# An encoder trunk on one core: the first norm by tiles, the first weight slab in halves, and two orders of work in the later norms

## The chip, the cores and the metric

The kernel runs on 1 core of one Trainium2 chip. Its engines are TensorE (PE), VectorE (DVE), ScalarE (ACT), GpSimd (POOL) and SyncE (SP, which only issues transfers). The metric is the device time of one execution in microseconds (us), the median of the runs.

## The reference, cut to what matters

Two layers of an encoder over x (1, 512, 1024), float32. Layer 0 mixes with RWKV-7 and spatial gating, layer 1 with differential attention; each then cross-attends into 256 memory tokens and ends in a gated MLP. Every sub-layer starts with the same norm and a projection:

```python
def rms_norm(x, gain):
    normed = x * lax.rsqrt(jnp.mean(x * x, axis=-1, keepdims=True) + 1e-6)
    return normed * gain

for l in range(2):
    h = rms_norm(x, mix_norm[l])
    if l == 0:
        z = h @ ab_w_in[0]          # (512, 1024) @ (1024, 2944): zf, zu, zv below
        ...
    x = x + memory_cross_attention(rms_norm(x, cross_norm[l]), ...)
    x = x + conv_gated_ffn(rms_norm(x, ffn_norm[l]), ffn_w_up[l], ..., ffn_w_down[l])
```

## The kernel before

**The products.** Weights come in slabs of 512 rows by 512 columns (`WRAW`, 128x2048 in SBUF, two buffers, loaded by SP in order; the load of slab i waits until slab i-2 is split). Each slab is split into a high part `WHI` (ScalarE, L332, rounds to fp32r) and a low part `WLO` = raw - high (VectorE, L338). Activations are split in the same way into `HIS` and `LOS`. A product is three matmuls (L372): high x high, high x low, low x high, each 128x512. A slab is 4 banks of PSUM x 4 steps x 3 = 48 matmuls. A product `zf` has four groups of banks, two slabs (`si` 0 and 1) each; groups use the same PSUM banks 0 to 3, so a group waits until the one before is evacuated. `gemm_pe` runs the matmuls, `gemm_side` the splits and evacuations on the other engines, up to three slabs ahead or to a given `limit`.

**The order.** Each engine runs a program written out by hand (`tensor_program`, `scalar_program`, `vector_program`, `pool_program`); they meet in semaphores that each count one kind of event (`sq`, `var`, `rstd`, `xn`, `tp`, `hi`, `lo` of a norm; `w_hi`, `w_lo` of the splits).

**A norm** works on four tiles of 128 tokens. ScalarE squares and sums a tile (L461, or in halves L499), VectorE makes the variance, GpSimd raises it to -0.5 (L473 for four columns, L505 for one), VectorE scales the tile (`XN`, L481 or L518). TensorE turns it: 8 transposes of 128x128 a tile, channel block k into bank k (L561, L576, L580). When a channel block has all four tiles (`tp`), ScalarE makes its high tile with the gain (L468) and VectorE its low tile (L487); the first matmul waits for the first low tile.

**The head** (norm `n0`) waits for all four sums at once (`norm_dve_front`), then turns channel by channel into banks 4 to 7 twice (`norm_pe`), so the second four wait for the first four low tiles. The gains come as a row tile `VROW`, turned by TensorE (L2067) and copied to `COLS` by VectorE (`setup_dve`, L2082). Four more row tiles are turned behind the norm (L2071) and give the `factors` (`factors_dve`, L2089 to L2098), for which TensorE and ScalarE wait before the first product. GpSimd issues ten loads of constants (`load_constants`, 2.3 MB) when the first weight slab has landed.

**The norms `nf0`, `nf1`, `n1`** follow a product whose last group fills four banks. `norm_tiles_pe` turns tiles 0 to 2 into the four banks that are free, then into the other four (when the last sum `ev` has been added), then tile 3 into all eight, with one `tp` per channel block. At `n1` the product `dn01` is followed by the product `dk`, whose first two slabs are split before the last four sums (L585) are added.

Of the kernel before, what the change touches and what calls it, by code (L numbers as in the profile page):

```python
# [19 lines left out]
F32 = mybir.dt.float32  # L20
# [5 lines left out]
P = 128  # L26
D = 1024
# [63 lines left out]
def build(nc, a, out):  # L91
# [473 lines left out]
    def norm_tiles_pe(T, tag, name, early):  # L565
# [4 lines left out]
        for ks in (range(early, early + 4), range(late, late + 4)):  # L570
            if ks[0] == late:
                e.wait_ge(*at(name, "ev", 2 * NT))
            for t in range(NT - 1):
                e.wait_ge(*at(tag, "xn", t + 1))
                for k in ks:
                    e.transpose(PS[:, k, t * P:t * P + P], XN[:, t, k * P:k * P + P], ident)  # L576
        t = NT - 1
        e.wait_ge(*at(tag, "xn", NT))
        for k in range(DC):
            e.transpose(PS[:, k, t * P:t * P + P], XN[:, t, k * P:k * P + P], ident).then_inc(sem(tag, "tp"), 1)  # L580
# [1481 lines left out]
    def setup_pe(T):  # L2062
# [3 lines left out]
        e.wait_ge(S("v_first"), V_FIRST)  # L2066
        e.transpose(PS[:, 0, 0:P], VROW[0][:, :], ident).then_inc(S("v_tp"), 1)  # L2067
        norm_pe(T, "n0", XN, NT, 4)
        e.wait_ge(S("v_in"), V_IN)
        for i in range(1, 5):  # L2070
            e.transpose(PS[:, 1, (i - 1) * P:i * P], VROW[i][:, :], ident).then_inc(S("v_tp"), 1)  # L2071
# [7 lines left out]
    def setup_dve(V):  # L2079

        V.e.wait_ge(S("v_tp"), 1)
        V.e.tensor_copy(COLS[:, 0:P], PS[:, 0, 0:P]).then_inc(S("cols"), 1)  # L2082
        V.e.wait_ge(S("cols"), 1)

    def factors_dve(V):
# [3 lines left out]
        V.mine(e.tensor_copy(COLS[:, P:5 * P], PS[:, 1, :]))  # L2089
# [42 lines left out]
    norm_shares("n0", NT)  # L2132
# [103 lines left out]
    def scalar_program(A):  # L2236
# [68 lines left out]
    def vector_program(V):  # L2305
# [21 lines left out]
        for l in range(2):  # L2327
# [155 lines left out]
```

## Time and profile before

| what | value |
|---|---|
| median of 3 runs | 1799.59 us (1798.09 to 1802.88) |
| the profiled execution's own time | 1797.6 us |
| its span, first to last instruction | 1795.8 us |
| mean granted TensorE clock | 0.994 of full |
| TensorE busy | 1730.6 us (96%) |
| VectorE, ScalarE, GpSimd busy | 953.6, 767.0, 177.2 us |

A busy time counts an engine's instructions whether or not anyone waits for them. All times in the trace count from the span's start. An instruction's row gives its start, its length and in brackets how long the engine stood before it and who ended that. A row may merge several instructions of one kind (x4); the length is then that of the whole run. Lengths of consecutive matmuls overlap; their pitch is the run's length by their number. In tables of windows the columns are the window's length, the busy us and number of instructions of PE, PEld (weight loads), DVE, ACT and POOL, then the granted TensorE clock (1.00 is 2.4 GHz, 0.50 is 1.2 GHz), the share of DMA engines busy, and GB/s.

### The profile page before, as it was taken

The page shows a single profiled execution, that of the slowest core. Times are in us where ns is not written, and L with a number is a line of the kernel's source. Part 1 is how long each engine was busy: PE and PEld are TensorE (multiplying, and loading weights), DVE is VectorE, ACT ScalarE, POOL GpSimd, SP SyncE. Part 2 cuts the span into 40 slices and gives each one's busy share as a digit, 9 for nine tenths or more (in the row PEclk, how much of TensorE's full clock was granted, in tenths as well). Part 3 has the DMA queues.
Part 4 walks back from the last instruction along what each step waited for, and adds up shares of the span by engine and source line. Part 5 has one row for each costly group of instructions (what it writes and reads, how often), then busy time and mean ns, then how long its engine had stood idle before and what let it go on. Part 6 is the DMA issues. An engine that isn't in the chain of part 4 may idle for free.

```text
span 1795.8 us, 29502 instructions
## 1 busy us (share of the span) xinstructions
PE 1730.6 (96%) x12913; PEld 1421.7 (79%) x12913; DVE 953.6 (53%) x1257; ACT 767.0 (43%) x1180; POOL 177.2 (10%) x179
## 2 busy tenths in 40 slices
PE   6998899999999999999999999999999999999999
PEld 5877787878887788888887887668887788888887
DVE  5478676545353566525644445875434456634552
ACT  4243555535553444314433235874654344412440
POOL 1001322130100000000000121440010000000000
PEclk9999999999999999999999999999999999999999
DMA  7210000143321332232322222003431233232331
GB/s 248 82 48 1 4 4 28 50 149 120 118 94 49 92 94 94 97 103 82 94 94 94 94 94 71 1 1 118 141 109 49 78 94 94 94 114 74 94 105 60
DMA packets 96444, 149.26 MB, mean 83 GB/s; under 512 B 3479, under 2 KB 50170, under 8 KB 96314
## 3 DMA queue, kind: packets, MB, share of 16 engines
q1 hardware_dynamic: 94727, 142.29, 24.4%
q0 software_dynamic: 1296, 4.95, 0.8%
q8 instruction: 102, 1.67, 0.4%
q14 instruction: 28, 0.23, 0.0%
q10 hardware_dynamic: 291, 0.12, 0.0%
HBM read 145.25 MB, written 2.10 MB: 82 GB/s over the span
## 4 chain that ended last, share of the span: by engine, by line
PE 86%; DVE 6%; ACT 4%; issue 2%; DMA 1%; POOL 1%; SPq 0%; POOLq 0%; ACTq 0%; DVEq 0%
PE PS L372 71%; PE PS L1646 1%; PE PS L1615 1%; DVE SS L1939 1%; PE PS L958 1%; PE PS L684 1%; DVE WLO L338 1%; PE PS L1770 1%; PE PS L1109 1%; PE PS L1071 1%; PE PS L1790 1%; DVE AT L1951 1%; ACT WHI L332 1%; PE PS L561 1%; PE PS L1095 1%
## 5 line engine op out<-in xcount | busy, mean ns | idle before, releaser
L338 DVE TENSOR_TENSOR WLO<-WRAW,WHI 128x2048 fp32r<-128x2048 f32 (+1 forms) x131 | 294.5, 2251 | 443.5 <-ACT WHI L332 443.5
L332 ACT ACTIVATE WHI<-WRAW 128x2048 fp32r<-128x2048 f32 (+1 forms) x132 | 248.4, 1882 | 396.7 <-PE PS L372 381.5
L372 PE MATMUL PS<-HIS,WHI 128*128 128x512 f32 x856 | 333.8, 390 | 3.3 <-DVE LOS L487 1.8
L372 PE MATMUL PS<-HIS,WLO 128*128 128x512 f32 x856 | 333.0, 389 | 0.0
L372 PE MATMUL PS<-LOS,WHI 128*128 128x512 f32 x856 | 333.0, 389 | 0.0
L372 PE MATMUL PS<-WHI,HIS 128*128 128x512 f32 x608 | 241.0, 396 | 0.9 <-DVE LOS L487 0.9
L372 PE MATMUL PS<-WHI,LOS 128*128 128x512 f32 x608 | 237.5, 391 | 0.0
L372 PE MATMUL PS<-WLO,HIS 128*128 128x512 f32 x608 | 237.4, 391 | 0.0
L372 PEld LDWEIGHTS PS<-HIS,WHI 128*128 128x128 f32 x856 | 160.7, 188 | 37.3 <-issue 2.4
L372 PEld LDWEIGHTS PS<-HIS,WLO 128*128 128x128 f32 x856 | 160.7, 188 | 33.5
L372 PEld LDWEIGHTS PS<-LOS,WHI 128*128 128x128 f32 x856 | 160.7, 188 | 33.4 <-issue 0.2
L372 PE MATMUL PS<-WHI,GHI 128*128 128x512 f32 x352 | 136.9, 389 | 0.0
L372 PE MATMUL PS<-WHI,GLO 128*128 128x512 f32 x352 | 136.9, 389 | 0.0
L372 PE MATMUL PS<-WLO,GHI 128*128 128x512 f32 x352 | 136.9, 389 | 0.0
L372 PEld LDWEIGHTS PS<-WHI,HIS 128*128 128x128 f32 x608 | 114.7, 189 | 26.8 <-issue 3.4
L372 PEld LDWEIGHTS PS<-WLO,HIS 128*128 128x128 f32 x608 | 114.7, 189 | 24.3
L372 PEld LDWEIGHTS PS<-WHI,LOS 128*128 128x128 f32 x608 | 114.8, 189 | 23.1
L585 DVE TENSOR_TENSOR X<-X,PS 128x512 f32<-128x512 f32 x64 | 43.0, 684 | 68.9 <-PE PS L372 68.8
L372 PEld LDWEIGHTS PS<-WHI,GLO 128*128 128x128 f32 x352 | 66.1, 188 | 13.8
L372 PEld LDWEIGHTS PS<-WHI,GHI 128*128 128x128 f32 x352 | 66.1, 188 | 13.7
L372 PEld LDWEIGHTS PS<-WLO,GHI 128*128 128x128 f32 x352 | 66.1, 188 | 13.7
L1732 ACT ACTIVATE GHI<-SG 128x512 fp32r<-128x512 f32 x44 | 27.8, 632 | 109.0 <-DVE SG L1752 109.0
(302 smaller groups left out, 2389.8 us busy)
## 6 DMA issues: line engine op xcount, KB each, us to landing
WRAW<-ffn_w_up SPq DMA_DIRECT2D x88, 512.0 KB, 4.7
WRAW<-ffn_w_down SPq DMA_DIRECT2D x20, 1024.0 KB, 5.0
WRAW<-cross_wkv SPq DMA_DIRECT2D x16, 1024.0 KB, 5.0
WRAW<-diff_w_in SPq DMA_DIRECT2D x12, 1024.0 KB, 5.1
WRAW<-ab_w_in SPq DMA_DIRECT2D x10, 1024.0 KB, 5.5
WRAW<-cross_wq SPq DMA_DIRECT2D x8, 1024.0 KB, 5.1
WRAW<-cross_wo SPq DMA_DIRECT2D x8, 1024.0 KB, 5.1
X<-x SPq DMA_DIRECT2D x8, 512.0 KB, 5.3
```

Source lines behind the costliest of these rows:

```text
L332: A.e.activation(part(WHI[place(i)], i), part(WRAW[i % 2], i), ACT.Copy).then_inc(S("w_hi"), 1)
L338: V.e.tensor_tensor(part(WLO[place(i)], i), part(WRAW[i % 2], i), part(WHI[place(i)], i).bitcast(F32), ALU.subtract).then_inc(S("w_lo"), 1)
L372: mm = e.matmul(o, l, r, start=(si == 0 and kk == 0 and q == 0), stop=(si == len(steps) - 1 and kk == nk - 1 and q == 2))
L561: mm = e.transpose(PS[:, norm_bank(b0, k), t * P:t * P + P], xn[:, t, k * P:k * P + P], ident)
L585: V.e.tensor_tensor(o, o, PS[:, bank_base(name, gi) + b, :], ALU.add).then_inc(sem(name, "ev"), 1)
L684: mm = e.transpose(PS[:, bank0 + k % 4, t * P:t * P + P], tok[:, t, k * P:k * P + P], ident)
L958: mm = e.matmul(PS[xs(x), b + hh, t * P:t * P + P].rearrange("p (s k) -> p s k", s=2), l[half(hh), d, chunk(t, x)], ar[half(hh), d, 0:2, c ...
L1071: mm = e.matmul(PS[xs(c), 2 * d + (x ^ c), q * CH:q * CH + CH], AI[xs(x), d, u, :], UU[xs(x), d, 2 * q + c, :], start=True, stop=True)
L1095: mm = e.matmul(PS[xs(x), 2 * d + (x ^ c), q * CH:q * CH + CH], TT[xs(c), d, 2 * q + x, :], XX[xs(c), d, 2 * q + (x ^ c), :], start=True, ...
L1109: mm = e.matmul(PS[xs(x), 2 * d + u // 4, (u % 4) * P:(u % 4) * P + P], UU[xs(x), d, u, :], AXT[xs(x), d, u, :], start=True, stop=True)
L1615: mm = e.matmul(PS[:, 4 * (t % 2) + h // 2, (h % 2) * MEM:(h % 2) * MEM + MEM], QFT[:, 2 * h + k, t * P:t * P + P], KFT[:, 2 * h + k, :], ...
L1732: A.e.activation(GHI[2 * gi + b - 2][:, :], SG[b - 2][:, :], ACT.Copy).then_inc(sem(name, "hi"), 1)
```

## The change

**Head.** The sums, variances, powers and scalings of `n0` go tile by tile (`first_norm_dve`, `norm_pool_tiles`). TensorE turns each tile into all eight banks as it comes (`setup_pe`); the gains' row goes into a corner of bank 7. The first slab's high part is made in two halves (`first_hi_act`), its first low half on VectorE, its second on GpSimd (`first_lo`). The first slab's product (`first_slab_pe`) no longer waits for the factors; it waits for each low tile, takes the second half of the slab when GpSimd is done, and turns the other four row tiles between its banks 1 and 2. The factors are made behind the split of slab 2, on VectorE; ScalarE waits for them before the first evacuation. GpSimd issues the constants' loads after its half.

**Norms `nf0`, `nf1`, `n1`.** Only tiles 0 and 1 are turned ahead; tiles 2 and 3 are turned together, channel block by channel block.

**`n1`.** VectorE's limit of splits before the last sums goes down by one slab: the second slab of `dk` is split after the norm's low tiles. ScalarE's limit stays.

```diff
@@ -570,14 +570,16 @@
         for ks in (range(early, early + 4), range(late, late + 4)):
             if ks[0] == late:
                 e.wait_ge(*at(name, "ev", 2 * NT))
-            for t in range(NT - 1):
+            for t in range(NT - 2):
                 e.wait_ge(*at(tag, "xn", t + 1))
                 for k in ks:
                     e.transpose(PS[:, k, t * P:t * P + P], XN[:, t, k * P:k * P + P], ident)
-        t = NT - 1
-        e.wait_ge(*at(tag, "xn", NT))
         for k in range(DC):
-            e.transpose(PS[:, k, t * P:t * P + P], XN[:, t, k * P:k * P + P], ident).then_inc(sem(tag, "tp"), 1)
+            for t in range(NT - 2, NT):
+                if k == 0:
+                    e.wait_ge(*at(tag, "xn", t + 1))
+                mm = e.transpose(PS[:, k, t * P:t * P + P], XN[:, t, k * P:k * P + P], ident)
+            mm.then_inc(sem(tag, "tp"), 1)
 
     def add_residual(V, name):
         def evac(gi, b, n):
@@ -2063,12 +2065,72 @@
 
         e = T.e
         e.wait_ge(S("ident_in"), 16)
-        e.wait_ge(S("v_first"), V_FIRST)
-        e.transpose(PS[:, 0, 0:P], VROW[0][:, :], ident).then_inc(S("v_tp"), 1)
-        norm_pe(T, "n0", XN, NT, 4)
+        for t in range(NT):
+            if t == NT - 1:
+                e.wait_ge(S("v_first"), V_FIRST)
+                e.transpose(PS[:, 7, 3 * P:4 * P], VROW[0][:, :], ident).then_inc(S("v_tp"), 1)
+            e.wait_ge(*at("n0", "xn", t + 1))
+            for k in range(DC):
+                if (t, k) == (NT - 1, DC - 1):
+                    e.wait_ge(S("cols"), 1)
+                mm = e.transpose(PS[:, k, t * P:t * P + P], XN[:, t, k * P:k * P + P], ident)
+                if t == NT - 1:
+                    mm.then_inc(sem("n0", "tp"), 1)
+
+    def first_slab_pe(T):
+
+        e = T.e
+        ready = lambda k: at("n0", "lo", k)
+        e.wait_ge(S("w_first_lo"), 1)
+        bank_pe(e, "zf", 0, 0, 0, [0, 1], hhi, hlo, tokens_out=False, ready=ready)
+        e.wait_ge(S("w_lo"), 1)
+        bank_pe(e, "zf", 0, 0, 0, [2, 3], hhi, hlo, tokens_out=False, ready=ready)
+        bank_pe(e, "zf", 0, 0, 1, range(4), hhi, hlo, tokens_out=False)
         e.wait_ge(S("v_in"), V_IN)
+        e.wait_ge(*at("n0", "lo", 5))
         for i in range(1, 5):
-            e.transpose(PS[:, 1, (i - 1) * P:i * P], VROW[i][:, :], ident).then_inc(S("v_tp"), 1)
+            e.transpose(PS[:, 4, (i - 1) * P:i * P], VROW[i][:, :], ident).then_inc(S("v_tp"), 1)
+        bank_pe(e, "zf", 0, 0, 2, range(4), hhi, hlo, tokens_out=False)
+        bank_pe(e, "zf", 0, 0, 3, range(4), hhi, hlo, tokens_out=False).then_inc(sem("zf", "wused"), 1)
+
+    def first_hi_act(A, h):
+        part_hi = A.e.activation(WHI[0][:, 2 * h:2 * h + 2, :], WRAW[0][:, 2 * h:2 * h + 2, :], ACT.Copy)
+        part_hi.then_inc(S("w_first_hi" if h == 0 else "w_hi"), 1)
+        A.split = h
+
+    def first_lo(E, h):
+        if h == 1:
+
+            E.e.wait_ge(S("w_first_lo"), 1)
+        E.e.wait_ge(S("w_first_hi" if h == 0 else "w_hi"), 1)
+        E.e.tensor_tensor(WLO[0][:, 2 * h:2 * h + 2, :], WRAW[0][:, 2 * h:2 * h + 2, :],
...
+
+    def first_hi_tile_act(A, k):
+        A.e.wait_ge(*at("n0", "tp", k + 1))
+        A.e.activation(HHI[k][:, :], PS[:, k, :], ACT.Copy, scale=col("mix_norm", k)).then_inc(sem("n0", "hi"), 1)
+
+    def first_lo_tile_dve(V, k):
+        V.e.wait_ge(*at("n0", "hi", k + 1))
+        V.e.scalar_tensor_tensor(HLO[k][:, :], PS[:, k, :], col("mix_norm", k), HHI[k][:, :].bitcast(F32),
+                                 ALU.mult, ALU.subtract).then_inc(sem("n0", "lo"), 1)
+
+    def first_var_dve(V, t):
+        V.e.wait_ge(*at("n0", "sq", t + 1))
+        V.e.tensor_scalar(SM[:, 4 + t:5 + t], SM[:, t:t + 1], 1.0 / D, EPS, ALU.mult, ALU.add)\
+            .then_inc(sem("n0", "var"), 1)
+
+    def first_norm_dve(V):
+
+        for t in range(2):
+            first_var_dve(V, t)
+            scale_tile_dve(V, "n0", t)
+        first_var_dve(V, 2)
+        first_var_dve(V, 3)
+        scale_tile_dve(V, "n0", 2)
+        scale_tile_dve(V, "n0", 3)
+        setup_dve(V)
 
     def setup_pool(G):
         G.mine(G.e.memset(SM[:, 24:25], 1e-12))
@@ -2079,14 +2141,14 @@
     def setup_dve(V):
 
         V.e.wait_ge(S("v_tp"), 1)
-        V.e.tensor_copy(COLS[:, 0:P], PS[:, 0, 0:P]).then_inc(S("cols"), 1)
+        V.e.tensor_copy(COLS[:, 0:P], PS[:, 7, 3 * P:4 * P]).then_inc(S("cols"), 1)
         V.e.wait_ge(S("cols"), 1)
 
     def factors_dve(V):
 
         e = V.e
         e.wait_ge(S("v_tp"), 5)
-        V.mine(e.tensor_copy(COLS[:, P:5 * P], PS[:, 1, :]))
+        V.mine(e.tensor_copy(COLS[:, P:5 * P], PS[:, 4, :]))
         V.wait_mine()
 
         V.mine(e.tensor_tensor(SM[:, 200:215], col("ab_shift_prev", 0, 15), col("ab_shift_next", 0, 15), ALU.add))
...
@@ -2195,8 +2257,9 @@
     def tensor_program(T):
         setup_pe(T)
 
-        T.e.wait_ge(S("factors"), 1)
-        gemm_pe(T, "zf", hhi, hlo, tokens_out=False, operand=lambda k: at("n0", "lo", k))
+        first_slab_pe(T)
+        gemm_pe(T, "zf", hhi, hlo, tokens_out=False, operand=lambda k: at("n0", "lo", k),
+                only=[(gi, si) for gi in range(4) for si in range(2) if gi + si > 0])
         gemm_pe(T, "zu", hhi, hlo, tokens_out=False, beside=zu_beside_pe(T))
         rw0_pe(T)
         gemm_pe(T, "zv", hhi, hlo)
@@ -2239,11 +2302,18 @@
 
         load_vectors(A.e, True)
         norm_act_front(A, "n0", X, SQ, NT, arrives=True)
-        split_hi(A, 1)
+        A.e.wait_ge(S("raw_in0"), raw_level[0])
+        first_hi_act(A, 0)
+        first_hi_act(A, 1)
         A.e.wait_ge(S("cols"), 1)
-        norm_act_back(A, "n0", NT, gcol("mix_norm", 0), hhi, 4)
-        A.e.wait_ge(S("factors"), 1)
-        side("zf", zf_act(A), fence)
+        for k in range(DC):
+            first_hi_tile_act(A, k)
+
+        def vectors(s):
+            if s == 1:
+                A.e.wait_ge(S("factors"), 1)
+
+        side("zf", zf_act(A), fence, vectors)
         lambda_act(A)
         side("zu", zu_act(A), fence, zu_beside_act(A))
         rw0_act(A)
@@ -2306,13 +2376,18 @@
         def side(name, evac=None, limit=None, beside=None):
             gemm_side(V, name, split_lo, evac, limit, beside)
 
-        norm_dve_front(V, "n0", X, XN, NT)
-        split_lo(V, 1)
-        setup_dve(V)
-        norm_dve_back(V, "n0", NT, gcol("mix_norm", 0), hhi, hlo, 4, 0, 4)
-        factors_dve(V)
-        norm_dve_back(V, "n0", NT, gcol("mix_norm", 0), hhi, hlo, 4, 4, DC)
-        side("zf", zf_dve(V), fence)
+        first_norm_dve(V)
+        first_lo(V, 0)
+        for k in range(DC):
+            first_lo_tile_dve(V, k)
+        V.e.wait_ge(S("w_lo"), 1)
+        V.split = 1
+
+        def vectors(s):
+            if s == 0:
+                factors_dve(V)
+
+        side("zf", zf_dve(V), fence, vectors)
         lambda_dve(V)
         side("zu", None, fence, zu_beside_dve(V))
         rw0_dve(V)
@@ -2357,15 +2432,15 @@
                 side(f"up{l}{h}", up_dve(V, l, h))
                 if (l, h) == (0, 1):
 
-                    side("dn01", residual_and_norm_dve(V, "dn01", "n1", close=True), gemms["dk"][0][0][1][0] + 1)
+                    side("dn01", residual_and_norm_dve(V, "dn01", "n1", close=True), gemms["dk"][0][0][0][0] + 1)
                 else:
                     side(f"dn{l}{h}", add_residual(V, f"dn{l}{h}"))
 
 
     def pool_program(G):
         setup_pool(G)
-        norm_pool(G, "n0", NT)
-        G.e.wait_ge(S("raw_in0"), 16)
+        norm_pool_tiles(G, "n0")
+        first_lo(G, 1)
         load_constants(G.e)
         rw0_pool(G)
         sgu_pool(G)
```

## Rows read from the trace of the kernel before

**Rows 1.** The page, part 4: the chain that ended last, shares by engine.

```profile
PE 86%; DVE 6%; ACT 4%; issue 2%; DMA 1%; POOL 1%; SPq 0%; POOLq 0%; ACTq 0%; DVEq 0%
```

**Rows 2.** The chain in order of time, 0 to 90 us: start, length, what.

```profile
24.43 65.58 PE PS L372 x288
```

**Rows 3.** Timeline of the head: start, length, engine, line, what [idle before <-releaser].

```profile
5.78 0.19 ACT L461 ACTIVATION_READ_ACCUMULATOR SQ<-X 128x1 f32 x1
...
12.02 2.74 DVE L481 TENSOR_SCALAR XN<-X,SM 128x1024 f32<-128x1024 f32 x4 [1.21 <-POOL SM L473]
...
12.62 1.91 ACT L332 ACTIVATE WHI<-WRAW 128x2048 fp32r<-128x2048 f32 x1 [2.01 <-DMA WRAW<-ab_w_in]
...
16.88 0.29 DVE L2082 COPY COLS<-PS 128x128 f32<-128x128 f32 x1
...
17.20 2.42 ACT L468 ACTIVATE HIS<-PS,COLS 128x512 fp32r<-128x512 f32 x4 [2.67 <-DVE COLS L2082]
...
18.01 2.73 DVE L487 SCALAR_TENSOR_TENSOR LOS<-PS,COLS,HIS 128x512 fp32r<-128x512 f32 x4 [0.84 <-ACT HIS L468]
...
18.82 3.68 PE L561 MATMUL PS<-KC,XN 128*128 128x128 f32 x16 [0.96 <-DVE LOS L487]
...
22.28 0.68 PE L2071 MATMUL PS<-KC,VROW 128*128 128x128 f32 x4
...
27.09 1.92 ACT L332 ACTIVATE WHI<-WRAW 128x2048 fp32r<-128x2048 f32 x1 [0.76 <-DMA WRAW<-ab_w_in]
```

**Rows 4.** GpSimd's groups by line and shape: busy us, mean ns | idle before.

```profile
L1369 POOL TENSOR_TENSOR BET<-KK,TMP 128x1024 f32<-128x1024 f32 x4 | 10.6, 2642 | 11.1 <-PE PS L1037 11.1
...
L505 POOL TENSOR_TENSOR SM<-SM 128x1 f32<-128x1 f32 x12 | 10.0, 885 | 561.7 <-DVE SM L513 561.6
...
L338 POOL TENSOR_TENSOR WLO<-WRAW,WHI 128x2048 fp32r<-128x2048 f32 x1 | 4.6, 4594 | 0.0
```

**Rows 5.** Timeline of VectorE beside GpSimd's L1369 (136.93 to 139.32), L338 (371.97 to 376.56).

```profile
137.56 2.30 DVE L757 TENSOR_TENSOR KK<-KK,SQN 128x512 f32<-128x512 f32 x1
...
372.66 0.28 DVE L991 TENSOR_TENSOR YL<-YL,PS 128x128 f32<-128x128 f32 x1
```

**Rows 6.** Timeline around norm nf0, VectorE and TensorE.

```profile
599.87 1.58 DVE L518 TENSOR_SCALAR XN<-X,SM 128x1024 f32<-128x1024 f32 x2 [0.16 <-POOL SM L505]
...
600.68 1.97 PE L576 MATMUL PS<-KC,XN 128*128 128x128 f32 x16 [0.53 <-DVE XN L518]
...
602.49 1.04 PE L580 MATMUL PS<-KC,XN 128*128 128x128 f32 x8
...
604.41 0.47 PE L372 MATMUL PS<-HIS,WHI 128*128 128x512 f32 x1 [0.89 <-DVE LOS L487]
```

**Rows 7.** Timeline around norm n1, VectorE and TensorE.

```profile
960.26 2.29 DVE L338 TENSOR_TENSOR WLO<-WRAW,WHI 128x2048 fp32r<-128x2048 f32 x1 [8.59 <-ACT WHI L332]
...
964.39 0.68 DVE L585 TENSOR_TENSOR X<-X,PS 128x512 f32<-128x512 f32 x1
...
966.60 0.66 PE L576 MATMUL PS<-KC,XN 128*128 128x128 f32 x4 [2.88 <-DVE XN L518]
...
966.63 2.40 DVE L518 TENSOR_SCALAR XN<-X,SM 128x1024 f32<-128x1024 f32 x3
...
967.44 4.27 PE L576 MATMUL PS<-KC,XN 128*128 128x128 f32 x20 [0.18 <-DVE XN L518]
...
973.47 0.47 PE L372 MATMUL PS<-WHI,HIS 128*128 128x512 f32 x1 [0.89 <-DVE LOS L487]
```

**Rows 8.** Windows: busy us of each engine, granted clock, DMA share, GB/s.

```profile
12.60:27.10 14.50, 11.28 (x48) 9.30 (x49) 11.33 (x22) 9.01 (x11) 5.97 (x10) 1.00 0.94 306
...
312.60:316.00 3.40, 3.40 (x74) 3.40 (x69) 3.40 (x6) 0.00 (x0) 0.00 (x0) 0.50 0.02 5
...
969.50:971.00 1.50, 1.50 (x9) 1.50 (x8) 0.00 (x0) 0.00 (x0) 0.00 (x0) 0.50 0.00 0
```

**Rows 9.** Timeline of TensorE in the pair stage.

```profile
311.76 1.49 PE L958 MATMUL PS<-AR,BET 64*64 64x128 f32 x36 [2.43 <-issue]
```

More of the change, by code:

```diff
@@ new lines, in first_hi_act @@
+    def first_hi_act(A, h):
[7 more added lines that the diff above has]
+        E.e.tensor_tensor(WLO[0][:, 2 * h:2 * h + 2, :], WRAW[0][:, 2 * h:2 * h + 2, :],
+                          WHI[0][:, 2 * h:2 * h + 2, :].bitcast(F32), ALU.subtract)\
+            .then_inc(S("w_first_lo" if h == 0 else "w_lo"), 1)
@@ L2124, in norm_shares @@
         n = nt if by_tile else 1
-        shares(tag, "norm", sq=2 * nt if by_tile else nt, var=n, rstd=n, xn=nt, tp=DC, hi=DC, lo=DC)
+        shares(tag, "norm", sq=2 * nt if by_tile and tag != "n0" else nt, var=n, rstd=n, xn=nt, tp=DC, hi=DC, lo=DC)
     def turn_shares(tag, nt):
@@ L2129, in turn_shares @@
         shares(tag, "turn", gvar=1 if tag == "do" else n, grstd=n, gn=DH if tag == "do" else nt, ttp=DC, tev=DC, hi=DC if tag == "do" else 0)
-    norm_shares("n0", NT)
+    norm_shares("n0", NT, True)
     for l in range(2):
```

## The prediction

> **What bounds the kernel now.** First the page's chain of work: 86% of it is TensorE [rows 1]. Time is won only where TensorE stands still or runs at half speed, and then only if nothing else is late next. The change touches four such places: the head (norm `n0` up to the first matmul) and three norms, `nf0`, `nf1` and `n1`.
>
> In the head the chain in order of time enters a run of 288 matmuls at 24.43 us, 65.58 us long, so 0.2277 us each, with no hole [rows 2]. What comes earlier at 24.43 moves the end. The timeline before it [rows 3] shows why it starts so late: the four sums are waited for together, a variance, one power on GpSimd (VectorE stands 1.21 us for it, from 10.81), four scalings until 14.76, a whole low part on VectorE, the column copy until 17.17, four high and low tiles, then 16 transposes whose banks those four had to free (18.82 to 22.50), four vector transposes, and a block of factors (22.96 to 24.43, 1.47 us). The weights had landed at 12.6: the high part that waited for them starts at 12.62.
>
> **The head after the change.** Each step starts some 0.05 us after its releaser.
>
> Tiles: the first square's sum is out at 5.97. Variance (0.2), hand-over (0.3), power and scaling follow per tile. A power of one column takes 0.89 us on average [rows 4], where the four-column one held VectorE 1.21; a scaling takes 0.69 (four in 2.74). Tile 0 is scaled by about 7.7, tile 1 by 9.3, tile 2 by 11.5. The last variance stays at 10.8, as before; its power meets tile 2's scaling and ends near 12, so tile 3 is scaled by 12.8 (before: 14.76). TensorE turns 8 blocks a tile: 16 transposes took 3.68 us, 0.213 us apart [rows 3], so it ends tile 2 at 13.2, the vector row at 13.4 and tile 3 at 15.1. The columns are copied by 14.15.
>
> High halves: a 128x2048 one takes 1.91 us, halves about 1.04 each, 12.62 to 14.65. Nothing of the change can precede the landing. High tile 0 follows at 14.65 to 15.34; the next are 0.58 apart (four in 2.42).
>
> Low parts: VectorE's half is 1.15 to 1.23 (half of the 2.20 to 2.29 us whole); it starts at 14.2 behind the column copy and ends at 15.4. Low tile 0 ends at 16.15, the others 0.68 apart (four in 2.73). So the first matmul is at **16.2**. Two steps, six matmuls, take 1.37.
>
> GpSimd's half is the new wait. It starts at 15.5. A whole low part there took 4.59 us once, so 2.30 for half; two-operand instructions of the same 128x1024 took 2.64 on average [rows 4]. I take 2.5: done at 18.0. TensorE stands 17.57 to 18.05, then does two steps (19.4), bank 1 (12 matmuls, 2.73) until 22.15, four vector transposes (0.44 to 0.85; I take 0.45 at full clock) until 22.6, banks 2 and 3 until **28.05**. Before, these 48 matmuls ended at 24.43 + 10.93 = 35.36. Gain **7.3 us**.
>
> Does GpSimd hinder VectorE? A VectorE product with both operands in SBUF took 2.30 us beside a GpSimd product, where 128x512 low tiles take 0.68; beside GpSimd's whole low part, VectorE instructions with one operand in PSUM took 0.28 each and started as their inputs came [rows 5]. The low tiles read PSUM and one SBUF tile, and VectorE's own half is over before GpSimd's begins. Nearest row: nothing. The other bound, held for all of it, is 2.5 us.
>
> The clock. The windows view says 1.00 throughout the head, but has no other evidence: the transposes' 0.213 us is the pitch that `n1` shows (20 in 4.27 us [rows 7]) where the granted clock is 0.50, so 1.2 GHz [rows 8], while `nf0` does 16 in 1.97 us [rows 6], twice as fast. So the head runs at 1.2 GHz until 22.4, and the last vector transposes are already fast (four in 0.68 us [rows 3]). It rose after 3.6 us of unbroken transposes. After the change TensorE turns from 7.7 to 15.1 with one hole of 0.35, which should raise it before the matmuls. But the faster the transposes end, the longer it stands until 16.2: up to 2.4 us. A hole of 2.43 us before 311.76 was followed, 0.8 us after work resumed, by a granted 0.50 for 3.4 us [rows 8, 9]. At half clock for such a stretch at the matmuls' start, 1.7 us would go, of which the waits for low tiles and for GpSimd hide up to 0.5. Bounds 0 and 1.7. I take 0.5: head **6.8 us**.
>
> In sentences of their own: the Trainium skill, "TensorE: Matmul & The Clock Gate", Part 4 (PE-mode transpose), says transposes do not count as busy for the clock as matmuls do, so full rate does not engage. This trace disagrees, since the rise at 22.4 came with only transposes behind it. By the page the first matmuls would be at half clock, and the sum would be that of the clock rival below.
>
> **What lies behind the head.** Slab 1 is split when the eight tiles are done: low tiles end at 20.9, its low part at 23.2; TensorE wants it at 28.05. Slab 2's load now waits for GpSimd's half (18.0, was 17.0), and GpSimd's ten constant loads (2.3 MB) are issued behind that half too, from 18.0 instead of 12.84. Before, slab 2 landed at 27.05 with the constants ahead of it [rows 3]; 306 GB/s was moved from 12.6 to 27.1 [rows 8]. Slab 2 and the constants, 3.4 MB, at that rate end by 29.1; slab 2 alone I put at 27. Behind its landing stand high part 2.0, low part 2.3, factors 1.5, slab 3's low part 2.3 and bank 0's evacuation 1.5, together 9.6; TensorE wants bank 0 at 28.05 + 10.93 = 39.0. So a landing up to 29.4 costs nothing, a later one us for us. The factors themselves, off the way to the first matmul, stand in that slack. `v_in` is due at 22.15, and was there by 22.28 before.
>
> **The three norms.** `nf0`: tile 3 is scaled at 601.45 (599.87 + 1.58), but TensorE is still on 16 transposes until 602.49, then turns tile 3; the first matmul follows at 604.41, 1.92 us after tile 3's first transpose [rows 6]. Of those 16, eight are tile 2's, which now go with tile 3's by channel, and eight, of tiles 0 and 1, need not wait for tile 2 (scaled at 600.66) any more. All that stands ahead of channel 0 is then over before 601.45, so it waits for tile 3 alone, at 601.5. The first matmul comes at 603.45. Gain 0.95. There are two such norms, and `nf1` repeats these rows 828.9 us later: **1.9 us**. Behind channel 0 a pair costs 0.22 us, against 0.59 for a high tile, so nothing comes late.
>
> `n1`: the low part of slab `dk` 1 (960.26 to 962.55) held back the first three sums; the last ended at 965.07, tile 3's scaling at 969.03 (966.63 + 2.40). TensorE's last matmul was over at 963.72; so with VectorE free the last sum ends at 964.4, and tile 3's scaling, 0.65 earlier, at 968.4. Before, the transposes ran at the 0.50 clock and reached tile 3 only at 971.54 (1.93 before the matmul). Now tile 3's first is at 968.45, the matmul 1.93 behind it at 970.4, where it was at 973.47: 3.1 us. If the clock falls all the same, matmuls at half speed from 970.4 cost up to 0.9: bounds 2.2 and 3.1. The hole before the transposes shrinks from 2.88 to some 1.6, so I take **2.7 us** [rows 7]. The moved low part runs behind the eight low tiles, 974.8 to 977.1, and is wanted at 970.4 + 10.9 = 981.3; its successor's load, issued behind it, lands 5 us later and is wanted at 1003.
>
> **Sum.** 6.8 + 1.9 + 2.7 = 11.4 us. The profiled execution took 1797.6 us around its span of 1795.8; it becomes 1786.2. The median of the runs, 1799.6, lies 2.0 above, so the forecast is **1788.2 us**.
>
> **Rivals.**
> *The clock stays at or falls to half at the first matmuls, in the head and in `n1`.* For: the fall after 2.43 us [rows 9]. Against: `n0`'s rise on transposes alone [rows 3], the shorter hole in `n1`. Head 7.3 less 1.7 to 3.4, `n1` 2.2: gain 8.0 to 9.7, time 1790 to 1791.6. Chance 0.22. (The page's rule named above would make it this one.)
> *GpSimd's half holds VectorE or lasts longer.* Low tile 0 would be at 18.7: gain 11.4 - 2.5 = 8.9, 1790.7. Chance 0.06.
> *Slab 2 lands late and TensorE stands at bank 0 of the second group.* At 240 GB/s shared evenly it would land at 32: 2.6 us lost, gain 8.8, 1790.8. Chance 0.05.
> *Nothing measurable.* The gain is given back in the stages between 90 and 400 us, where waits and clock falls follow each other. For: falls there depend on where holes come. Against: every wait there is relative to the work before. 1797 to 1801. Chance 0.07.
> *Slower.* The landing of slab 2 again, as one mechanism: it would have to come after 29.4 + 11.4 + 5.4 = 46 us for a loss over 0.3%. That is a rate below 120 GB/s for 3.4 MB, against 306. 1805 or more. Chance 0.02.
> The forecast keeps 0.58.
>
> Below 0.3%, 5.4 us, a difference can't be told from none here. Faster: 0.58 + 0.22 + 0.06 + 0.05 = 0.91; same 0.07, slower 0.02. The range: both upper bounds give 12.3 us, 1787.3, less 1.5 that the runs spread below their median: 1785.8. Above, the clock rival's 1791.6 and 1.4 of spread: 1793.
>
> **What would show it.** First matmul near 16.2, a hole of half a us at 17.6, slab 0 over near 28; the low tiles at 0.68 while GpSimd works; no wait of TensorE for an evacuation near 39; the first matmul 1.9 us behind tile 3's first transpose in the norms, and no 0.50 stretch in `n1`. Wrong if the first matmuls are 0.43 us apart, or if GpSimd's half or slab 2 come late.

## The result

| | before | changed |
|---|---|---|
| median of 9 runs each | 1797.38 us (1795.46 to 1802.88) | 1786.89 us (1783.05 to 1793.63) |
| ratio of the runs, 95% interval | | 0.9942 (0.9922 to 0.9961) |
| profiled execution | 1797.6 us | 1787.84 us |
| its span | 1795.8 us | 1786.0 us |
| mean granted TensorE clock | 0.994 | 0.996 |

The change makes the kernel 0.58% faster, 10.5 us by the medians, 9.8 by the two spans. The forecast was 1788.2 us, from a gain of 11.4 over the 1799.6 us of the first three runs; the median of all nine lies 2.2 us lower.

The page of the changed kernel, part 4, where [rows 1] had TensorE at 86%:

```profile
PE 85%; DVE 6%; ACT 5%; issue 2%; DMA 2%; POOL 1%; POOLq 0%; SPq 0%; DVEq 0%; ACTq 0%
```

The timeline of its head, against [rows 2, 3] (start, length, engine, line, what, idle before and who ended it):

```profile
7.63 3.45 PE L2076 MATMUL PS<-KC,XN 128*128 128x128 f32 x16 [7.63 <-DVE XN L518]
...
11.35 1.09 PE L2076 MATMUL PS<-KC,XN 128*128 128x128 f32 x8 [0.27 <-DVE XN L518]
...
12.26 2.00 ACT L2097 ACTIVATE WHI<-WRAW 128x1024 fp32r<-128x1024 f32 x2 [1.81 <-DMA WRAW<-ab_w_in]
...
12.54 1.09 PE L2076 MATMUL PS<-KC,XN 128*128 128x128 f32 x8
...
13.43 1.23 DVE L2106 TENSOR_TENSOR WLO<-WRAW,WHI 128x1024 fp32r<-128x1024 f32 x1 [0.55 <-ACT WHI L2097]
14.17 4.72 ACT L2112 ACTIVATE HIS<-PS,COLS 128x512 fp32r<-128x512 f32 x8
14.73 2.38 POOL L2106 TENSOR_TENSOR WLO<-WRAW,WHI 128x1024 fp32r<-128x1024 f32 x1 [3.04 <-DVE WLO L2106]
14.87 5.36 DVE L2116 SCALAR_TENSOR_TENSOR LOS<-PS,COLS,HIS 128x512 fp32r<-128x512 f32 x8 [0.22 <-ACT HIS L2112]
...
15.77 0.47 PE L372 MATMUL PS<-HIS,WHI 128*128 128x512 f32 x1 [2.14 <-DVE LOS L2116]
```

The reader sees: the weights' first high half starts at 12.26 when the load lands; the first matmul follows 3.51 us behind it, at 15.77. The eight low tiles take 5.36 us, 0.67 each, though GpSimd's half runs beside them from 14.73 to 17.11: it does not hold VectorE. The transposes start 0.213 us apart at first and 0.109 apart behind 10.7 us.

Further on in the same timeline:

```profile
17.05 0.73 POOL L2050 DMA_DIRECT2D RC<-rkc  x1
...
22.27 0.57 POOL L2058 DMA_DIRECT2D LAM<-diff_lambda_k  x1
...
25.00 1.92 ACT L332 ACTIVATE WHI<-WRAW 128x2048 fp32r<-128x2048 f32 x1 [4.30 <-DMA WRAW<-ab_w_in]
...
33.82 1.92 ACT L332 ACTIVATE WHI<-WRAW 128x2048 fp32r<-128x2048 f32 x1 [6.90 <-DMA WRAW<-ab_w_in]
...
35.77 2.29 DVE L338 TENSOR_TENSOR WLO<-WRAW,WHI 128x2048 fp32r<-128x2048 f32 x1 [5.23 <-ACT WHI L332]
...
38.76 0.75 DVE L715 SCALAR_TENSOR_TENSOR ZS<-PS,COLS,ZS 128x511 f32<-128x511 f32 x1
...
39.65 0.47 PE L372 MATMUL PS<-HIS,WHI 128*128 128x512 f32 x1 [1.33 <-DVE ZS L715]
```

The table of TensorE's waits from 20 to 100 us has one row (us in total, times, longest):

```profile
PE PS L372 <- DVE ZS L715: 1.3, 1, 1.3
```

This is the wait that took the place of the one removed. GpSimd issues its ten loads from 17.05 to 22.8. Slab 2 landed at 25.0. Slab 3's load, issued behind slab 1's split, lands only at 33.7. Its high part (ScalarE) and then its low part (VectorE) stand ahead of bank 0's evacuation, and TensorE stands for that evacuation before its second group. The chain in order of time has it as one piece, 10.61 us from the load's issue, where the page before had loads of this kind at a median of 5.5:

```profile
23.12 10.61 DMA WRAW<-ab_w_in
```

The table of the DMA queues from 23.1 to 29 us (packets, MB, share of 16 engines) shows whose bytes moved in the meantime: q0 carries GpSimd's constants, q1 the weights.

```profile
q0 software_dynamic: 528, 1.61, 93.2%
q1 hardware_dynamic: 131, 0.24, 12.7%
```

The norms `nf0` and `n1`, against [rows 6, 7], in the timeline; the last line is the window of `n1` (columns as in [rows 8]):

```profile
596.65 1.86 PE L581 MATMUL PS<-KC,XN 128*128 128x128 f32 x15 [0.37 <-DVE XN L518]
...
598.64 0.47 PE L372 MATMUL PS<-HIS,WHI 128*128 128x512 f32 x1
```

```profile
959.66 0.66 PE L576 MATMUL PS<-KC,XN 128*128 128x128 f32 x4 [1.69 <-DVE XN L518]
...
962.22 2.14 PE L581 MATMUL PS<-KC,XN 128*128 128x128 f32 x16
...
964.49 0.47 PE L372 MATMUL PS<-WHI,HIS 128*128 128x512 f32 x1
```

```profile
957.90:964.50 6.60, 4.24 (x34) 3.48 (x33) 4.92 (x10) 2.60 (x7) 2.94 (x4) 1.00 0.00 0
```

At `nf0` TensorE waits for tile 3 alone (0.37 us) and multiplies 1.99 us behind it. At `n1` its hole shrank from 2.88 to 1.69 us and the clock stayed at 2.4 GHz.

**All stages side by side.** From the starts of the matmuls of L372, in us: the first high half, the first matmul, slab 0 and slab 1 of `zf` (first matmul to first matmul), the pair stage (last matmul of `zv` to first of `ab`), `ab` to the last of `xo0`, and each norm (last matmul before it to the first behind it). The parts between are alike within 0.3 us everywhere. The last column is the time in us that the clock spent at 0.50 after a fall: before 24 us (the start, before the first rise, not counted), in the pair stage, and from `ab` to `xo0`. The rows e1 to e11 are the experiments below.

| kernel | high half | matmul | slab 0 | slab 1 | pair | ab to xo0 | nf0 | n1 | nf1 | at 0.50 |
|---|---|---|---|---|---|---|---|---|---|---|
| before | 12.62 | 24.43 | 11.02 | 10.88 | 205.90 | 236.11 | 6.87 | 10.14 | 6.87 | 0, 11.3, 5.7 |
| changed | 12.26 | 15.77 | 11.51 | 12.37 | 208.67 | 235.06 | 5.95 | 6.90 | 5.95 | 0, 10.2, 3.4 |
| e1 | 12.85 | 16.36 | 13.12 | 10.88 | 208.20 | 237.34 | 5.95 | 8.11 | 5.95 | 3.4, 12.3, 8.2 |
| e2 | 11.98 | 24.30 | 11.01 | 10.88 | 205.37 | 233.59 | 5.95 | 6.90 | 5.95 | 0, 10.2, 0 |
| e3 | 11.43 | 14.94 | 11.78 | 12.23 | 206.55 | 235.14 | 6.87 | 10.21 | 6.87 | 0, 10.2, 3.4 |
| e4 | 11.97 | 16.95 | 12.90 | 10.88 | 206.37 | 240.57 | 5.95 | 7.96 | 5.95 | 3.4, 12.0, 15.3 |
| e5 | 11.63 | 15.50 | 11.84 | 12.57 | 206.80 | 235.19 | 5.96 | 6.90 | 5.95 | 0, 10.2, 3.4 |
| e6 | 11.43 | 14.94 | 11.53 | 10.88 | 207.01 | 239.01 | 5.96 | 6.90 | 5.95 | 0, 11.6, 8.9 |
| e7 | 12.31 | 23.22 | 11.01 | 10.88 | 205.14 | 236.20 | 5.96 | 7.74 | 5.96 | 0, 11.1, 6.0 |
| e8 | 11.69 | 22.76 | 11.04 | 10.88 | 207.32 | 235.18 | 6.88 | 7.82 | 6.87 | 0, 10.2, 3.4 |
| e9 | 11.98 | 16.44 | 13.04 | 10.88 | 208.15 | 236.06 | 5.95 | 6.90 | 5.95 | 3.4, 6.8, 3.4 |
| e10 | 11.89 | 15.78 | 11.84 | 10.88 | 208.61 | 241.93 | 5.95 | 6.90 | 5.95 | 0, 11.9, 15.4 |
| e11 | 11.66 | 15.66 | 11.87 | 10.88 | 208.16 | 238.68 | 5.95 | 6.89 | 5.95 | 0, 10.2, 6.8 |

Before against changed, the rows add up: first matmul -8.66, slab 0 +0.49, slab 1 +1.49, pair stage +2.77, ab to xo0 -1.05, norms -0.92, -3.24 and -0.92, the rest +0.3; in all -9.8, the difference of the spans.

**The new heads side by side**, in us, with e4 and e9 (both low halves on VectorE) and e10 and e11 (transposes added) explained below. The columns: when the clock first rises to 2.4 GHz, how far the first matmul lies behind the start of the first high half, how long TensorE stands between its last transpose and that matmul, and when the clock falls again.

| kernel | rise | matmul behind high half | TensorE stands | fall |
|---|---|---|---|---|
| changed | 10.7 | 3.51 | 2.14 | none |
| e1 | 11.0 | 3.51 | 2.40 | 17.8 |
| e3 | 11.6 | 3.51 | 1.59 | none |
| e4 | 13.2 | 4.98 | 2.76 | 16.6 |
| e5 | 12.9 | 3.87 | 1.52 | none |
| e6 | 10.9 | 3.51 | 1.88 | none |
| e9 | 11.0 | 4.46 | 3.00 | 17.8 |
| e10 | 13.3 | 3.88 | 0 | none |
| e11 | 13.0 | 3.99 | 0 | none |

Two things can be read from it. The three falls come behind the three longest stands (2.40 to 3.00 us; up to 2.14 none followed). And where the clock rose only at 12.9 or later, the first matmul comes some 0.4 to 0.5 us late: the transposes, 0.21 us apart for longer, hold up the turned row of gains, so VectorE copies the columns only behind it and starts its low half late. In e5 the copy starts 1.5 us behind the high half; in the changed kernel 0.3 us.

```profile
13.14 0.29 DVE L2144 COPY COLS<-PS 128x128 f32<-128x128 f32 x1 [1.19 <-PE PS L2071]
```

### The profile page after: what moved, and what is told of

The parts are those of the page before. It is cut to its first block, busy times and chain, and to the rows that moved or that the text cites. A ratio compares the mean times of both kernels' runs of the same rounds, so it can differ in the third digit from the quotient of the medians.

```text
span 1786.0 us, 29514 instructions
## 1 busy us (share of the span) xinstructions
PE 1726.1 (97%) x12913; PEld 1417.9 (79%) x12913; DVE 953.3 (53%) x1260; ACT 766.3 (43%) x1181; POOL 181.0 (10%) x183
## 4 chain that ended last, share of the span: by engine, by line
PE 85%; DVE 6%; ACT 5%; issue 2%; DMA 2%; POOL 1%; POOLq 0%; SPq 0%; DVEq 0%; ACTq 0%
PE PS L372 70%; PE PS L1648 1%; DVE SS L1941 1%; PE PS L1617 1%; PE PS L960 1%; PE PS L686 1%; DVE WLO L338 1%; PE PS L1111 1%; PE PS L1073 1%; ACT WHI L332 1%; DVE AT L1953 1%; PE PS L1772 1%; PE PS L1792 1%; PE PS L1097 1%; DMA WRAW<-ab_w_in 1%
## 5 line engine op out<-in xcount | busy, mean ns | idle before, releaser
L338 DVE TENSOR_TENSOR WLO<-WRAW,WHI 128x2048 fp32r<-128x2048 f32 (+2 forms) x130 | 292.2, 2250 | 434.3 <-ACT WHI L332 434.3
L372 PE MATMUL PS<-HIS,WHI 128*128 128x512 f32 x856 | 334.0, 390 | 3.7 <-DVE LOS L2116 2.1
L372 PE MATMUL PS<-HIS,WLO 128*128 128x512 f32 x856 | 333.1, 389 | 0.0
L372 PE MATMUL PS<-LOS,WHI 128*128 128x512 f32 x856 | 333.0, 389 | 0.0
L372 PE MATMUL PS<-WHI,HIS 128*128 128x512 f32 x608 | 240.5, 396 | 0.1
L372 PE MATMUL PS<-WLO,HIS 128*128 128x512 f32 x608 | 237.2, 390 | 0.0
L372 PE MATMUL PS<-WHI,LOS 128*128 128x512 f32 x608 | 237.0, 390 | 0.0
L372 PEld LDWEIGHTS PS<-HIS,WHI 128*128 128x128 f32 x856 | 160.6, 188 | 38.5 <-issue 5.0
L372 PEld LDWEIGHTS PS<-LOS,WHI 128*128 128x128 f32 x856 | 160.7, 188 | 33.3 <-issue 0.2
L372 PEld LDWEIGHTS PS<-HIS,WLO 128*128 128x128 f32 x856 | 160.7, 188 | 33.3
L372 PE MATMUL PS<-WHI,GHI 128*128 128x512 f32 x352 | 136.9, 389 | 0.0
L372 PE MATMUL PS<-WHI,GLO 128*128 128x512 f32 x352 | 136.9, 389 | 0.0
L372 PE MATMUL PS<-WLO,GHI 128*128 128x512 f32 x352 | 136.9, 389 | 0.0
L372 PEld LDWEIGHTS PS<-WHI,HIS 128*128 128x128 f32 x608 | 114.4, 188 | 26.0 <-issue 2.6
L372 PEld LDWEIGHTS PS<-WLO,HIS 128*128 128x128 f32 x608 | 114.4, 188 | 24.3
L372 PEld LDWEIGHTS PS<-WHI,LOS 128*128 128x128 f32 x608 | 114.5, 188 | 23.0
L372 PEld LDWEIGHTS PS<-WHI,GHI 128*128 128x128 f32 x352 | 66.1, 188 | 13.8
L372 PEld LDWEIGHTS PS<-WHI,GLO 128*128 128x128 f32 x352 | 66.1, 188 | 13.7
L372 PEld LDWEIGHTS PS<-WLO,GHI 128*128 128x128 f32 x352 | 66.1, 188 | 13.6
```

The source lines that it names most:

```text
L338: V.e.tensor_tensor(part(WLO[place(i)], i), part(WRAW[i % 2], i), part(WHI[place(i)], i).bitcast(F32), ALU.subtract).then_inc(S("w_lo"), 1)
L372: mm = e.matmul(o, l, r, start=(si == 0 and kk == 0 and q == 0), stop=(si == len(steps) - 1 and kk == nk - 1 and q == 2))
```

## The experiments

**e1: the constants' loads late.** Two theories of the hole before 39.65: slab 3's late landing behind the constants, or the order of VectorE's work by itself.

```diff
         first_lo(G, 1)
+        G.e.wait_ge(S("w_lo"), 4)
         load_constants(G.e)
```

> The changed kernel, but GpSimd issues the ten loads of constants only when slab 3's low part is done. Theory (the loads of slabs 2 and 3 share the transfer engines with 2.3 MB of constants, slab 3 takes 10.7 us to land, and its split stands ahead of the first evacuations, so TensorE stands 1.3 us for bank 0 of the second group): slab 3 lands within 6 us of its issue, TensorE has no hole near 38 us, the second group starts near 38.0 instead of 39.65, and the kernel gains 1.6 us over the changed one (about 12 us, ratio 0.9933, over the kernel before). Rival (the order on VectorE, factors and two splits ahead of the evacuation, is late by itself): slab 3 lands early, but bank 0 is still evacuated near 39.5 and the hole stays.

Measured: median 1787.39 us (7 runs), ratio 0.9947 (0.9928 to 0.9965). In the timeline:

```profile
29.68 1.92 ACT L332 ACTIVATE WHI<-WRAW 128x2048 fp32r<-128x2048 f32 x1 [5.02 <-PE PS L372]
...
34.23 0.73 POOL L2050 DMA_DIRECT2D RC<-rkc  x1 [16.53 <-DVE WLO L338]
```

Slab 3's high part no longer waits for the load (landed at 28.9) but for TensorE to leave slab 0, and slab 1 takes 10.88 us, without a hole: the theory holds for the place. VectorE's order is the same here, so it is not late by itself; as slab 0 itself was slow in this profile, e6, where it was not, is the cleaner proof. The gain did not show in the time. For the profiled run the window tells why (granted clock in the third column from the end):

```profile
17.80:21.20 3.40, 3.40 (x9) 2.72 (x9) 3.02 (x5) 3.40 (x4) 0.00 (x0) 0.51 0.66 205
```

This run had the clock at half for 3.4 us just behind the first matmuls, and slab 0 took 13.12 us instead of 11.5: the clock rival, worth 1.6 us, in the head; and 1.2 us once more in `n1` (8.11 instead of 6.90).

**e2: the norms alone**, **e3: the head alone.** The kernel before with the new `norm_tiles_pe` and the new limit, and the changed kernel with both as before.

> The kernel before with the change of the three norms alone (last two tiles by channels, and the second dk slab split after the norm's low tiles). Theory: nf0 gains 1.0, n1 3.2, nf1 0.8 us, in all 5.0, ratio 0.9972; n1 shows no 0.50 clock. Rival (the gain of n1 in the changed kernel was that one run's clock): n1 shows a fall of the clock here and gains about 2.2.

> The changed kernel with the three norms as before, so the head alone. Theory: slab 0 ends 8.3 us earlier, the second group starts 6.7 earlier, and the waits in the stages from 160 to 390 us take 0 to 3 of it: 4 to 6.7 us, ratio 0.996 to 0.998. If the loss in those stages (2.9 us in the profile of the changed kernel) belongs to the shifted head, it shows here and not in the kernel with the norms alone; if it is the run's own, it differs from profile to profile without regard to the head.

Measured: e2 1791.86 us, ratio 0.9972 (0.9955 to 0.9989), the expected figure, with `n1` at 6.90 and no fall there. e3 1791.57 us, ratio 0.9965 (0.9952 to 0.9978): 6.3 us of 1797.3 by the ratio, 5.7 by the medians, both in what was expected (4 to 6.7); its hole at the second group is there (slab 1 12.23). The two parts add to 0.9937 against 0.9942 together. The pair stage took 205.37 without the new head and 206.55 with it.

**e4: both low halves on VectorE.**

```diff
         first_lo(V, 0)
+        first_lo(V, 1)
...
-        first_lo(G, 1)
+        G.e.wait_ge(S("w_lo"), 1)
         load_constants(G.e)
```

> The changed kernel, but VectorE makes both low halves of slab 0 and GpSimd only waits for them before it issues the constants. Theory: the first low tile and the first matmul are 1.15 us later (16.9 instead of 15.77), slab 0 ends 1.15 later, but slab 3's landing behind the constants is what the second group waits for, so its start moves by less than 0.5 us and the time is that of the changed kernel. Rival (GpSimd's half is worth its 1.15 us): the second group starts 1.15 us later too, ratio 0.0006 higher.

Measured: 1789.47 us, ratio 0.9957 (0.9944 to 0.9969). The first matmul came at 16.95, 4.98 us behind the first high half instead of 3.51. That is 1.47 more where 1.15 was expected, but the late rise of the clock (13.2) is in it: against e5, with a rise at 12.9, it is 1.11. The clock fell at 16.6 for 3.4 us, slab 0 took 12.90, and with the second group wanted only at 40.73, slab 3 at 33.2 was early enough: no hole. So the hole exists only when what lies ahead of it is quick. The second group started 1.1 us later than in the changed kernel, more than the 0.5 expected, but behind a fall that had made slab 0 some 1.4 us longer. Whether VectorE's half costs anything net this run can't say; its interval overlaps the changed kernel's.

**e5: the changed kernel again**, **e6: the constants late again**, on one chip.

> The changed kernel itself once more, with a new profile, beside the next run on the same chip. Theory (the place of the holes in the instruction stream and of the clock's falls between 160 and 390 us is the run's own): the stretch from the last matmul of zv to the first of ab, 208.7 us in the first profile of this kernel and 205.9 before, differs from 208.7 by over 1 us. Rival (the changed kernel has these holes always): it is 208.2 to 209.2 again. Either way the hole of 1.3 us at the second group is there, since slab 3 lands 10 us or more after its issue, and the first matmuls are at half clock or not by chance (two of four heads so far).

> The kernel with the constants' loads behind slab 3's split once more, on the chip of the changed kernel. Theory: 1.6 us faster than the changed kernel, if both are compared at the same falls of the clock: lowest times 1.5 to 2 us apart (1781.1 against 1783.1 so far). Rival (what the second group wins is lost in the stages behind it): medians and lowest times equal within 0.5 us.

Measured: e5 1787.24 us (1783.38 to 1791.87), ratio 0.9941 (0.9921 to 0.9961); e6 1786.22 us (1783.38 to 1787.62), ratio 0.9929 (0.9914 to 0.9944). In the profiles slab 1 takes 12.57 in e5, with the hole (1.5 us), and 10.88 in e6, where slab 0 ran at full clock (11.53). With the constants early, the loss in slab 1 is there in every profile without a fall ahead (1.5 in the first, 1.3 in e3, 1.7 in e5). In the times it is not shown: 1.0 us lies between the medians, the lowest times are equal (the expected 1.5 to 2 missed), and the intervals overlap. Slab 3's load still waits to land in e6, but lands 6.2 us behind its issue at 22.29:

```profile
28.61 1.92 ACT L332 ACTIVATE WHI<-WRAW 128x2048 fp32r<-128x2048 f32 x1 [5.05 <-DMA WRAW<-ab_w_in]
```

The pair stage took 206.80 in e5, 1.9 us less than in the first profile of the same kernel, as the theory had it (over 1 us). In e5's slab 0 TensorE also waited for GpSimd's half: its third step starts 0.50 us behind the matmul before it, where the pitch is 0.23.

**e7: tiles by channel alone**, **e8: sums first alone**, each on the kernel before.

> The kernel before with tiles 2 and 3 of nf0, nf1 and n1 turned together, the second dk slab split where it was. Theory: nf0 and nf1 gain 0.9 each from tile 3's scaling to the first matmul; n1 (10.14 us from the last matmul to the first, before) gains what its transposes kept TensorE busy after tile 3 was scaled, 2.4 us with the clock at full or half, so 7.7 us. Rival (the order of transposes counts little at n1, the sums do it): n1 9 us or more.

> The kernel before with only the second dk slab's low part moved behind the norm's low tiles. Theory: the last sum and tile 3's scaling at n1 are 0.65 us earlier, and TensorE's hole before the first transpose shrinks from 2.88 to about 1.6 us; with the old order of transposes the first matmul is 1.3 us earlier at half clock and 3 us at full clock, so n1 7.1 to 8.8 us of 10.14. Rival (the moved split comes late): TensorE waits for the second dk slab 10.9 us after the first.

Timeline of TensorE at `n1` in e7, then in e8:

```profile
963.79 0.66 PE L576 MATMUL PS<-KC,XN 128*128 128x128 f32 x4 [2.88 <-DVE XN L518]
...
966.00 2.14 PE L581 MATMUL PS<-KC,XN 128*128 128x128 f32 x16
...
968.26 0.47 PE L372 MATMUL PS<-WHI,HIS 128*128 128x512 f32 x1
```

```profile
964.23 0.66 PE L576 MATMUL PS<-KC,XN 128*128 128x128 f32 x4 [1.69 <-DVE XN L518]
...
968.04 1.04 PE L580 MATMUL PS<-KC,XN 128*128 128x128 f32 x8
...
969.97 0.47 PE L372 MATMUL PS<-WHI,HIS 128*128 128x512 f32 x1 [0.89 <-DVE LOS L487]
```

e7 took 1791.45 us and e8 1793.98 us, one run each, too few to show a gain of this size; the profiles show it. `n1` took 7.74 (7.7 expected) and 7.82 us (7.1 at full clock to 8.8 at half; it ran at full), where the two profiles with the old `n1` have 10.14 (before) and 10.21 (e3). e7 keeps the hole of 2.88 and had no fall of the clock here; e8 has the shorter hole, 1.69. Both together reach 6.90. So the parts gain 2.4 and 2.3 alone and 3.2 together, and they overlap: one takes transposes out from behind tile 3's scaling, the other brings that scaling forward. Both profiles with the old `n1` have a fall of the clock in it, and neither e7 nor e8 has, so how much of each gain is the order and how much the clock isn't shown. The moved split was never waited for: slab 1 of `dk` follows slab 0 without a hole.

**e9: e4 with the constants late.**

> The changed kernel with both low halves of slab 0 on VectorE and the constants' loads behind slab 3's split. Theory (GpSimd's half takes VectorE's second 1.15 us off the way and adds no wait, and nothing behind gives that back when the constants are late): counted from the landing of slab 0 (the start of its first high half), the first matmul comes 4.65 to 4.75 us later (3.5 to 3.51 with GpSimd's half), slab 0 takes 11.5 at full clock or about 13 with a fall, and slab 1 takes 10.88, without a hole. Rival (GpSimd's half was itself a wait): slab 0 takes 11.0, half a us less than with it.

Measured: 1788.86 us (one run), first matmul 4.46 us behind the first high half (4.65 expected at least), so GpSimd's half brings it 0.95 us forward, at the same early rise of the clock, and 1.11 by e4 against e5, where the clock rose late. Slab 0 took 13.04 with a fall at 17.8, like e1's 13.12 with GpSimd's half; the rival (slab 0 half a us shorter without it) was for full clock, which this profile did not have, and stays untested.

**e10, e11: the hole before the first matmul filled.** The constants late, and

```diff
                     e.wait_ge(S("cols"), 1)
+                    for _ in range(14):
+                        e.transpose(PS[:, k, t * P:t * P + P], XN[:, t, k * P:k * P + P], ident)
                 mm = e.transpose(PS[:, k, t * P:t * P + P], XN[:, t, k * P:k * P + P], ident)
```

> The kernel with the constants late, in which TensorE writes the last block of tile 3 (channel block 7) fourteen times more before it reports it, so that it works from the end of the transposes nearly to the first matmul (1.5 us at full clock, 3.0 at half; the block is wanted only 3 us later). Theory (the falls at the first matmuls, in three of seven heads, come from the 2.1 us in which TensorE stands there): no fall before 150 us, first matmul 3.5 us behind the start of the first high half as without it, slab 0 in 11.5 us or less, and a median up to 0.7 us below that of the constants-late kernel, which this can't tell from none. Rival (the fall comes from something else): a fall near 17 us again, slab 0 in 13 us. Second rival: the extra work is at half clock and pushes the first matmul to 4.5 us behind.

> The same kernel once more for a second profile. Theory: again no fall at the first matmuls; with three of seven heads falling without the extra work, two heads without a fall would still come by chance one time in three, so only a fall decides, against the theory.

```profile
13.42 0.29 DVE L2146 COPY COLS<-PS 128x128 f32<-128x128 f32 x1 [1.20 <-PE PS L2071]
...
14.01 1.69 PE L2077 MATMUL PS<-KC,XN 128*128 128x128 f32 x14
...
14.88 5.36 DVE L2118 SCALAR_TENSOR_TENSOR LOS<-PS,COLS,HIS 128x512 fp32r<-128x512 f32 x8
...
15.54 0.27 PE L2078 MATMUL PS<-KC,XN 128*128 128x128 f32 x1
15.78 0.47 PE L372 MATMUL PS<-HIS,WHI 128*128 128x512 f32 x1
```

Neither had a fall ahead of 150 us, which three of the seven new heads with the hole had (e1, e4, e9 against the changed kernel, e3, e5, e6). By chance two would come without one every third time, so this does not settle it. The first matmul came 3.9 and 4.0 us behind the high half, where 3.5 was expected, but the extra transposes did not push it: the columns' copy was late before they began (13.42, behind a late rise of the clock), e5 has 3.87 without them, and the first low tile is followed 0.90 us later by the first matmul, as in the changed kernel (14.87 and 15.77). Filling the hole cost nothing here. e10's median is 1790.17 us, ratio 0.9946 (0.9927 to 0.9965), and e11's one run took 1789.28: no version here beats the changed kernel by more than the runs scatter.

## Why the prediction was right, point by point

The forecast of 1788.2 us was within 1.3 us of the median; not all its terms were. Part of that closeness is luck: the gain came out 0.9 us smaller than forecast (10.5 for 11.4), and the base, a median of three runs, lay 2.2 us above that of nine, which sets the time off the other way.

*The first matmul.* Forecast 16.2, found 15.77; the load landed 0.36 earlier than in the profile of before, and the chain behind it took 3.51 us for 3.58. Each step is near where it was put. GpSimd's half began at 14.73, where the forecast had 15.5, took 2.38 (2.5), did not hold VectorE, and was over at 17.11. The third step began at 17.24, in the usual pitch, so the forecast's hole of half a us did not appear in this profile. It did, at about 0.3 us, in e3, e5, e10 and e11, whose slab 0 took 11.78 to 11.87. That the columns' copy could be late when the clock rises late (e4, e5, e10, e11: 0.4 to 0.5 us) the forecast did not have; in the profile of the changed kernel it rose early.

*The end of slab 0.* 27.28 for 28.05: gain 8.2 instead of 7.3.

*The clock.* The forecast took 0.5 us off, between 0 and 1.7. In the profile nothing was lost, in e1, e4 and e9 a fall cost some 1.4 to 1.6. So the rival is no rival but an event: it came in three of seven such heads, those in which TensorE had stood longest (2.40, 2.76 and 3.00 us, against 1.52, 1.59, 1.88 and 2.14). Two of the three also have both halves on VectorE, which lengthens the stand. Length alone does not decide everywhere: at `n1` the hole of 1.69 us was followed by a fall in two of ten profiles (e1, e4), and that of 2.88 us in two of three (not in e7).

The rule named in the prediction, that transposes don't bring full rate (the Trainium skill, "TensorE: Matmul & The Clock Gate", Part 4), is contradicted again: the pitch of transposes halves at 10.7 us, from 0.213 to 0.109 us, with no matmul run yet but transposes, and slab 0's matmuls start 0.23 us apart (0.43 at half clock in e1).

*What lies behind the head.* Here a step failed. The prediction reckoned slab 2's landing (27; it was 25.0) against its slack. It counted slab 3's low part in the same row, but not slab 3's own landing. The constants' bytes, though issued from 17.05 on, began to move only at 20.7, so that slab 2, issued at 17.1, was hurt less than forecast and slab 3, issued at 23.1, stood behind them: from 23.1 to 29 us they moved 1.61 MB and the weights' queue 0.24. Its load took 10.6 us. From 33.8 on its high part (1.9), its low part (2.2) and bank 0's evacuation (1.5, with hand-overs 5.8 in all) end at 39.6, and TensorE was free at 38.3; 32.5 was the last moment for the landing. The "slab 2 late" rival had the right place, the wrong slab, and with 2.6 us nearly twice the price (1.3 to 1.5). e1 and e6 show the cause: with the constants later, the hole is gone.

*The second group's start, net:* 6.7 us earlier (46.33 to 39.65), where 6.8 was forecast. This agreement is luck, two errors that cancel: 1.4 us better up to slab 0's end (0.9 there, 0.5 for the clock), 1.5 us lost in slab 1.

*`nf0`, `nf1`.* 0.92 each for 0.95, in every profile with the new order.

*`n1`.* 3.24 instead of 2.7, just over the upper bound of 3.1: the last sum moved forward, the hole shrank to 1.69 (1.6 forecast), no fall. In e1 and e4 the clock fell at `n1` all the same and it took 8.11 and 7.96, a gain of 2.0 to 2.2, about the lower bound (2.2).

*The stages between.* The prediction gave "given back between 90 and 400 us" 0.07. It is there in part. The pair stage took 205.1 to 207.3 us in the four profiles with the old head (mean 205.9) and 206.4 to 208.7 in the nine with the new (mean 207.6); what grows are holes that end with nothing the profile shows (10.5 to 12.9 us in all with the old head, mean 11.5; 11.6 to 14.3 with the new, mean 12.7), such as this of the changed kernel:

```profile
221.43 0.27 PE L1073 MATMUL PS<-UU,AI 64*64 64x64 f32 x1 [0.77 <-issue]
```

Two profiles of the same kernel differ by 1.9 us, so neither "always" nor "the run's own" holds alone. Why a shorter head should lengthen them, or whether it is the changed instruction stream, wasn't tested and stays open. From `ab` to `xo0` the time mostly follows the clock: 233.59 us without a fall, 235.1 with 3.4 us at half, 236 with 6, up to 241.9 with 15.4. In e6, e9 and e11 it is 0.8 to 1.7 us longer than half the time at half clock accounts for. Among the profiles this stage varies by 8.3 us, the pair stage by 3.5. Of the runs only the mean granted clock is known, and it goes with their time (0.997 at 1783.05 us, 0.991 at 1791.64, both of the changed kernel; correlation -0.89 or stronger in every kernel of five or more runs). So most of the scatter of 10 us between runs is the clock's; that it arises in this stage is what the profiles suggest.

## What to carry to other kernels

A late start of the main stream is a chain: find its one fixed end (here the landing of the first weights), make everything else end beside it, and move behind it what only needs to be done soon. Then follow every load that is now issued closer to others, not the first alone: the saved time is lost at the next place where the loads' slack was. Where two orders of work hide behind the same event, price them together; their gains don't add.

## What was not expected of the hardware

The same hole can be followed by a fall of the granted clock in one run and by none in another: at `n1`, 1.69 us of standing were followed by 3.4 us at half in two of ten profiles. In the head the falls came behind the longest stands, and one of them costs some 1.5 us. The clock's first rise, at 10.7 to 13.3 us in the new heads, moves the first matmul by up to half a us. From `ab` to `xo0`, where the programs are the same, the profiles show 0 to 15.4 us at half clock, worth up to 8 us. And the ten loads from GpSimd's queue (2.3 MB) did not delay the 1 MB load issued beside their start (issued 17.1, landed 25.0) as much as the one issued behind the last of them: 7.8 us against 10.6. In e6, without them, slab 2 took 5.3 and slab 3 6.2.
